# Router products on raw x by token, best two among 8 columns, and a tenth place in the ring

## The chip, the cores and the metric

One Trainium2 chip, of which the kernel uses one core. The metric is the device time of one execution in microseconds (us), lower is better; the kernel before was run three times. A core has TensorE (PE; its weight loads are PEld), VectorE (DVE), ScalarE (ACT), GpSimd (POOL) and SyncE (SP), which only issues transfers here, and 16 DMA engines. All data are float32.

## The reference

One layer of a decoder for 256 prompt tokens and 8 sample tokens (D = 1024), cut to what the change touches:

```python
x = x + merge_branches(pool_out, att, gate_logits, w_up_pool, w_up_att, w_out)
h = rmsnorm(x, norm_ffn)
gl = h @ w_rg + b_rg                                  # 4 groups
g_idx, g_w = argmax(gl), softmax(gl)[argmax]
el = einsum('nd,gde->nge', h, w_re) + b_re            # 4 x 8 experts
el_sel = el[:, g_idx]                                 # the 8 of the chosen group
top_v, top_i = top_k(el_sel, 2); top_w = softmax(top_v)
gate = g_w * one_hot(g_idx) * sum(top_w * one_hot(top_i))
for w1, w3, w2, ge in 32 experts:
    acc += ge * ((silu(h @ w1) * (h @ w3)) @ w2)
y = rmsnorm(x + acc, norm_final)
```

Ahead of it stand an input projection (u, q, k, v, forget logits and 16 gate blocks of 128 columns), a pooling branch, attention over the prompt, and for each sample token attention over 1024 cached rows read through a page table.

## The kernel before

The weights pass through a ring of nine places of 2 MB (`slot`, one `ring` tensor). In the first part places 0 to 5 hold the input projection's weights, key pages (K), value pages (V), the up projections and w_out; 6 to 8 hold working tensors. `PLAN` is one list of steps that all engines walk in the same order, each doing its own share of a step: `proj` and `gate` (projection blocks on PE, copied out by ACT), `keys` (32 steps on DVE: one product with the broadcast query L1004 and one sum L1006 each, four for each sample token), `scores`, `smax`, `hnorm`, `pT`, `pv` (prompt attention), `snew` (the new key of the samples), `m1`, `dmax`, `dshift` (maximum over pages), `dpv`, `datt` (sample attention), `up`, `merge`, `out` (w_out), `norm` and `route`. What a step loads into a place is issued when the last use of its predecessor is over: by SP for weights and for the query broadcasts `qb`, by POOL for pages (`gather_pages`), in the order of the list. POOL also packs the router weights `wre`, `wrg` into `wr`, behind the step `psum` 3, when the five loads that ACT issues in `router_loads` (step `nat` of V) are in.

After `out`, for x of blocks 0 and 1 (128 tokens each) and the sample block 2: squares and root on ACT (L682, L687), a refinement of the root (L883 to L887) and `h2 = x * root` on DVE (L891), transposes of `h2` on PE (L1291, L1294), copies with the norm weights into `hT` on DVE (L904), router products with `wr` as the loaded side, 36 x tokens (L1584, L1591), bias on DVE, transposes back to tokens (L1598), then `route`: argmax over 4 groups, a mask of -1e30 on the experts of other groups, two rounds of argmax over 32 columns (`first_of_equals`, L1093 to L1097, five dependent instructions on 3 x 32 columns), ranks of the tokens in their experts by products with a triangle of ones (L1608), the first token gather (L1316). `inject` (L1306, L1308) puts x into the output accumulators in PSUM; `keep_warm` (L1369) is a product whose result nobody reads.

Then 32 experts: gather the tokens, transpose them, gate and up products (L1333), hidden values, down products (L1349), return to the tokens. Expert e uses places 3(e mod 3) to 3(e mod 3) + 2. SP loads the nine matrices of experts 0 to 2 as the places come free, in the order `FREED` of their last use, and further ones when the gate and up (`s_gu`) or the down products (`s_dn`) of expert e - 3 are done. Expert 31's matrices come in parts, and a final norm ends the kernel.

## Time and profile before

| | us |
|---|---|
| three runs | 736.56, 735.04, 734.88 (median 735.04) |
| profiled execution, whole | 734.89 |
| its span | 733.1 |
| PE busy in the span | 602.4 (82%) |
| DVE busy | 226.0 (31%) |
| ACT busy | 83.8 (11%) |
| POOL busy | 47.3 (6%) |
| moved by DMA | 269.13 MB, mean 367 GB/s |
| matrices of experts, 2048 KB each | 96 |

The span is the profiled stretch of the core; 1.8 us of the execution lie around it. Busy time of PE is not a measure of its being the limit, as products are pipelined; the slices, the stretches, the queue of SP and the chain of work that ended last (followed back from the last instruction to what released each one) say what each part waits for. In a timeline a row is a run of like instructions, with the idle time ahead of it and its releaser in brackets.

### The profile page before, as it was taken

What the parts mean: (1) busy time and instruction counts of PE and PEld (TensorE: products, weight loads), DVE (VectorE), ACT (ScalarE), POOL (GpSimd) and SP (SyncE); (2) the same over time, 40 slices, a digit from 0 to 9 for tenths busy, and PEclk for the clock granted to TensorE, in tenths of its full rate; (3) what the DMA queues carried; (4) which work ended last, traced back from release to release, by engine and by line L of the source; (5) the groups of instructions that cost most, each with busy time, mean ns of one, the idle gap of its engine ahead of it and who ended that gap; (6) DMA issues with size and microseconds to landing.
All of it is one profiled execution on the core that took longest, in us unless ns stands there. A gap on an engine that the chain in (4) does not pass through costs nothing.

```text
span 733.1 us, 13747 instructions
## 1 busy us (share of the span) xinstructions
PE 602.4 (82%) x6164; PEld 368.6 (50%) x6164; DVE 226.0 (31%) x550; ACT 83.8 (11%) x224; POOL 47.3 (6%) x58
## 2 busy tenths in 40 slices
PE   4899999999999999998667786778767676778774
PEld 3678777775574455554334443344334343444342
DVE  4249689972131462321111111111111111111113
ACT  2211142221101201000000000000000000000003
POOL 4106430112000000000000000000000000000000
PEclk8799999999999999999888898778988898889898
DMA  9967969997999456999999999999999999999992
GB/s 299 301 249 242 251 245 396 295 398 306 414 422 414 169 234 250 426 428 425 422 421 426 427 422 422 427 425 424 425 426 426 424 422 426 425 425 422 424 371 91
DMA packets 36602, 269.13 MB, mean 367 GB/s; under 512 B 5076, under 2 KB 5896, under 8 KB 18103
## 3 DMA queue, kind: packets, MB, share of 16 engines
q1 hardware_dynamic: 29824, 230.91, 78.4%
q0 software_dynamic: 3072, 35.19, 11.9%
q10 hardware_dynamic: 3647, 2.14, 1.0%
q8 instruction: 50, 0.82, 0.4%
q14 instruction: 9, 0.07, 0.0%
HBM read 265.99 MB, written 2.46 MB: 366 GB/s over the span
## 4 chain that ended last, share of the span: by engine, by line
DMA 49%; PE 47%; DVE 1%; ACT 1%; issue 1%; SPq 0%; ACTq 0%; DVEq 0%
DMA ring<-w_up 46%; PE bank L1333 9%; PE bank L1416 8%; PE bank L1508 8%; PE bank L1554 4%; PE bank L1569 4%; DMA wf<-w_in 3%; PE bank L1485 2%; PE bank L1349 1%; PE bank L1316 1%; PE bank L1364 1%; PE bank L1492 1%; PE bank L1369 1%; PE bank L1519 1%; PE bank L1523 1%
## 5 line engine op out<-in xcount | busy, mean ns | idle before, releaser
L1333 PE MATMUL bank<-ring,front 128*32 128x256 f32 x2048 | 163.4, 489 | 100.6 <-DMA ring<-w_up 97.0
L1333 PEld LDWEIGHTS bank<-ring,front 128*32 128x32 f32 x2048 | 89.7, 139 | 166.6 <-issue 142.6
L1192 DVE COPY front<-bank 128x256 f32<-128x256 f32 x32 | 13.6, 425 | 241.7 <-PE bank L1333 241.7
L1349 PE MATMUL bank<-ring,front 128*32 128x256 f32 x1024 | 61.2, 379 | 0.0
L1416 PE MATMUL bank<-hT,ring 128*128 128x264 f32 x256 | 60.9, 398 | 0.0
L1508 PE MATMUL bank<-hT,ring 128*128 128x264 f32 x256 | 59.7, 389 | 0.4 <-ACT front L758 0.4
L1416 PEld LDWEIGHTS bank<-hT,ring 128*128 128x128 f32 x256 | 49.5, 196 | 9.9 <-issue 1.2
L1316 PE MATMUL bank<-front 128*32 128x256 f32 (+1 forms) x768 | 53.0, 390 | 0.3 <-DVE front L1103 0.3
L1508 PEld LDWEIGHTS bank<-hT,ring 128*128 128x128 f32 x256 | 47.8, 190 | 9.7 <-issue 2.1
L815 ACT ACTIVATE front<-bank 128x128 f32<-128x128 f32 x32 | 8.9, 277 | 377.1 <-PE bank L1341 377.1
L1349 PEld LDWEIGHTS bank<-ring,front 128*32 128x32 f32 x1024 | 33.1, 110 | 22.1 <-issue 0.5
L1004 DVE TENSOR_TENSOR ring<-ring,front 128x1024 f32<-128x1024 f32 x32 | 40.4, 1263 | 4.3 <-DMA front<-q_scratch 4.2
L1202 DVE COPY front<-bank 128x256 f32<-128x256 f32 x32 | 13.6, 424 | 86.7 <-PE bank L1349 86.7
L1006 DVE TENSOR_REDUCE front<-ring 128x16 f32<-128x1024 f32 x32 | 39.0, 1220 | 1.1
L1364 PE MATMUL bank<-front 32*128 32x256 f32 x512 | 36.7, 400 | 0.0
L1316 PEld LDWEIGHTS bank<-front 128*32 128x32 f32 (+1 forms) x768 | 18.4, 108 | 24.7 <-issue 18.6
L1364 PEld LDWEIGHTS bank<-front 32*128 32x128 f32 x512 | 23.1, 184 | 13.9 <-issue 13.2
L1569 PE MATMUL bank<-ring,hT 128*128 128x512 f32 x64 | 28.3, 597 | 0.0
L1197 DVE TENSOR_TENSOR front<-front,bank 128x128 f32<-128x128 f32 x32 | 9.2, 287 | 41.8 <-ACT front L815 41.8
L1358 PE MATMUL bank<-front 128*32 128x256 f32 x256 | 20.0, 380 | 1.1 <-DVE front L1202 1.1
L1569 PEld LDWEIGHTS bank<-ring,hT 128*128 128x128 f32 x64 | 11.9, 190 | 16.4 <-issue 16.4
L820 ACT COPY front<-bank 128x256 f32<-128x256 f32 x32 | 11.9, 372 | 45.0 <-PE bank L1316 45.0
(293 smaller groups left out, 488.2 us busy)
## 6 DMA issues: line engine op xcount, KB each, us to landing
ring<-w_gate SPq DMA_DIRECT2D x31, 2048.0 KB, 33.8
ring<-w_down SPq DMA_DIRECT2D x31, 2048.0 KB, 38.5
ring<-w_up SPq DMA_DIRECT2D x31, 2048.0 KB, 38.3
ring<-w_in SPq DMA_DIRECT2D x8, 2048.0 KB, 22.9
ring<-w_out SPq DMA_DIRECT2D x2, 2048.0 KB, 16.8
front<-q_scratch SPq DMA_DIRECT2D x8, 256.0 KB, 7.8
ring<-w_up_pool SPq DMA_DIRECT2D x1, 2048.0 KB, 30.5
ring<-w_up_att SPq DMA_DIRECT2D x1, 2048.0 KB, 15.7
```

Of the source, the lines that this page charges most:

```text
L1004: v.tensor_tensor(ks, ks, qb[:, b % 2].unsqueeze(1).to_broadcast([P, 2, DC]), ALU.mult).then_inc(s_kprod, 1)
L1006: v.tensor_reduce(scs[:, b, 2 * pair:2 * pair + 2], ks.rearrange("p j (h d) -> p j h d", h=HEADS), AX.X, ALU.add).then_inc(s_kused, 1)
L1316: last = m.matmul(bank[GATHER][CAP * g:CAP * (g + 1), 0:QUART], sel[0:n, i, b], h2[0:n, b, g * QUART:(g + 1) * QUART], start=b == 2, stop= ...
L1333: last = m.matmul(bank[GATEUP][32 * g:32 * g + 32, 0:256], xgT[:, k % 2, k // 2], w[:, k, 256 * (g % 2):256 * (g % 2) + 256], start=k == 0 ...
L1349: last = m.matmul(bank[TDOWN][32 * g:32 * g + 32, 0:256], hE[:, j % 2, j // 2], wd[:, j, 256 * g:256 * g + 256], start=j == 0, stop=j == F ...
L1358: last = m.matmul(bank[SACC][CAP * g:CAP * (g + 1), 0:QUART], back[:, i, SEQ + CAP * g:SEQ + CAP * (g + 1)], ysb[:, i], start=False, stop= ...
L1364: last = m.matmul(acc[:, g, b], back[rows, i, b * P:(b + 1) * P], ysb[rows, i], start=False, stop=False, skip_group_check=True)
L1416: last = m.matmul(out[:, 0:TOK], w, hT[:, k, 0:TOK], start=k == 0, stop=k == DK - 1)
L1485: last = m.matmul(out[g:g + HEADS, :], scs[:, a, j], pages[:, j], start=j < 4, stop=j >= 4)
L1508: last = m.matmul(out[:, 0:TOK], w[:, k, cols], hT[:, k, 0:TOK], start=k == 0, stop=k == DK - 1)
L1554: last = m.matmul(out[:, 0:TOK], w[:, k, a * P:(a + 1) * P], src[:, k], start=k == 0, stop=k == CC - 1)
L1569: last = m.matmul(out[:], hT[:, k, b * P:(b + 1) * P], w[k // CC][:, k % CC, half * 512:(half + 1) * 512], start=k == 0, stop=k == DK - 1)
```

## The change

- **Ring.** `x` moves into a tenth place of 4096 columns (`x9`), together with `samp`, `unew` and the scratch for squares. After x is injected and normalised, that place takes expert matrices. Places are handed out in the order `FREED`, matrix n to place n mod 10; matrix n waits for the use of matrix n - 10. The final norm's results go into a place that is no longer needed.
- **Router.** x itself is transposed, among the products with w_out, and copied by ACT (one quarter by DVE). The router weights are loaded with rows (k p), in runs of 8 and 4 floats, and multiplied by the norm weights on POOL; they are now the moved side, so that logits stand by token. Root and bias are applied behind the product. ACT writes `h2` of block 1.
- **Choice.** The 8 logits of the chosen group are selected into 8 columns, both argmax rounds run on 3 x 8 columns, and the results are spread over 32 again. `turned(0)` stands earlier. Sample rows are 8 instead of 128 in rank and table products.
- **Order ahead of it.** `forgetT` one projection later; the product of new keys split off (`sprod`) ahead of `snew`; key steps one earlier. The query broadcasts of sample tokens 2 to 7 are issued by ACT at the second key step of the token before, no longer by SP. One more small load for the norm weights.

```diff
-NSLOT = 9
-NB = NSLOT // 3
+RING = 9
+NSLOT = RING + 1
+LAST = EXPERTS - 1
+ORDER = [(e, m) for e in range(LAST - 1) for m in range(3)] + [(LAST - 1, 0), (LAST - 1, 1), (LAST, 0), (LAST, 1), (LAST - 1, 2), (LAST, 2)]
...
+        x9 = sb("x9", [P, SLOT])
+        slot = [ring[:, n * SLOT:(n + 1) * SLOT] for n in range(RING)] + [x9[:]]
+        x = x9[:, 0:3 * D].rearrange("p (b n) -> p b n", b=3)
+        samp, unew = x9[:, 3 * D:3 * D + DC], x9[:, 3 * D + DC:4 * D]
...
-        PLAN += V[:1] + [("nat", C_K)] + keys(2)[:1] + V[1:2] + [("snew", 0)] + keys(2)[1:2] + V[2:3] + [("scores", 0)] + keys(2)[2:] + V[3:] + [("smax", 0)]
+        PLAN += V[:1] + [("nat", C_K), ("sprod", 0)] + keys(2)[:2] + V[1:2] + keys(2)[2:] + [("snew", 0)] + V[2:3] + [("scores", 0)] + keys(3)[:1] + V[3:] + [("smax", 0)]
-        KEYS_AT = (12, 13, 15, 17, 18, 19, 21, 23, 25, 26, 28, 30, 31, 32)
+        KEYS_AT = (13, 14, 16, 18, 19, 20, 22, 24, 26, 27, 28, 30, 31, 32)
...
+        home = {item: FREED[n % NSLOT] for n, item in enumerate(ORDER)}
+        arrived = {item: SLOT_BASE[home[item]] + 16 * (n // NSLOT + 1) for n, item in enumerate(ORDER)}
...
+                elif q == 8:
+                    sp.wait_ge(s_merge, DK)
                 else:
-                    sp.wait_ge(s_merge, DK)
-                load_matrix(sp, q // 3, q % 3, q)
+                    sp.wait_ge(s_inj, 1)
+                    sp.wait_ge(s_h2, 1)
+                load_matrix(sp, *ORDER[n], q)
+            def slot_used(n):
+                e, m = ORDER[n - NSLOT]
+                sp.wait_ge(s_gu if m < 2 else s_dn, e + 1)
...
-                    pool.wait_ge(in_route, 16 * 5)
-                    g.tensor_copy(wr[:, :, 0:EXPERTS].rearrange("p k (g e) -> p k g e", g=GROUPS), wre[:].rearrange("p g (k e) -> p k g e", k=DK)).then_inc(s_wr, 1)
-                    g.tensor_copy(wr[:, :, EXPERTS:], wrg[:].rearrange("p (k g) -> p k g", k=DK)).then_inc(s_wr, 1)
+                    pool.wait_ge(in_route, 16 * (GROUPS + 4))
+                    pool.wait_ge(*count_taken("pool"))
+                    g.tensor_tensor(wr[:], wr[:], nffnK.unsqueeze(2).to_broadcast([P, DK, EXPERTS + GROUPS]), ALU.mult).then_inc(s_wr, 1)
...
-                act.dma_start(wre[:], t["w_router_expert"][0].rearrange("g (p k) e -> p g (k e)", p=P)).then_inc(in_route, 16)
-                act.dma_start(wrg[:], t["w_router_group"][0].rearrange("(p k) g -> p (k g)", p=P)).then_inc(in_route, 16)
+                for g in range(GROUPS):
+                    act.dma_start(wr[:, :, g * PER_GROUP:(g + 1) * PER_GROUP], t["w_router_expert"][0, g].rearrange("(k p) e -> p k e", p=P)).then_inc(in_route, 16)
+                act.dma_start(wr[:, :, EXPERTS:], t["w_router_group"][0].rearrange("(k p) g -> p k g", p=P)).then_inc(in_route, 16)
...
+                elif step == "keys" and a % 4 == QROW_AT and a // 4 + 1 in range(2, NS):
+                    b = a // 4 + 1
+                    act.wait_ge(s_kprod, 4 * (b - 1))
+                    act.dma_start(qb[:, b % 2], qd[b].partition_broadcast(P)).then_inc(s_qb[b % 2], 16)
...
                 elif step == "norm":
...
+                    for half in range(2):
+                        s.copy(hT[:, 4 * half:4 * half + 4, 0:P], full("hT", 1 + half)[:].rearrange("p (k t) -> p k t", k=4)).then_inc(taken[TPOSE[1 + half][0]], 1)
...
+                    act.wait_ge(s_hsum, 1)
+                    s.activation(root[:, 1], rowsq[:, 1], ACT.Sqrt, bias=eps).then_inc(s_rt, 1)
+                    act.wait_ge(s_hsum, 2)
+                    s.activation(h2[:, 1].rearrange("t (k p) -> t p k", k=DK), x[:, 1].rearrange("t (p k) -> t p k", k=DK), ACT.Copy, scale=root[:, 1]).then_inc(s_h2, 1)
...
             def route():
                 src = full("logits")
-                link(v.memset(lgT[0:36, TOK:3 * P], 0.0))
-                v.tensor_scalar(lgT[0:36, 0:TOK], src[0:36, 0:TOK], br[:, 0:1], None, ALU.add).then_inc(taken[PART], 1)
+                v.scalar_tensor_tensor(lg[:, 1], src[:, 0:36], root[:, 1], br[:], ALU.mult, ALU.add).then_inc(taken[PART], 1)
...
-                first_of_equals(e1, em, r_m1, EXPERTS, ra)
-                link(v.scalar_tensor_tensor(em, e1, -2 * BIG, em, ALU.mult, ALU.add))
-                first_of_equals(e2, em, r_m2, EXPERTS, ra)
+                link(v.tensor_tensor(ra.rearrange("p b (g e) -> p b g e", g=GROUPS), lg[:, :, 0:EXPERTS].rearrange("p b (g e) -> p b g e", g=GROUPS), by_group, ALU.mult))
+                link(v.tensor_reduce(em8, ra.rearrange("p b (g e) -> p b e g", g=GROUPS), AX.X, ALU.add))
+                first_of_equals(first8, em8, r_m1, PER_GROUP, ra8)
+                link(v.scalar_tensor_tensor(em8, first8, -2 * BIG, em8, ALU.mult, ALU.add))
+                first_of_equals(top8, em8, r_m2, PER_GROUP, ra8)
...
                         for k in range(DK):
+                            if (i, k) == (3, 4):
+                                transposes(3)
                             last = m.matmul(out[:], hT[:, k, b * P:(b + 1) * P], w[k // CC][:, k % CC, half * 512:(half + 1) * 512], start=k == 0, stop=k == DK - 1)
...
+                        if i == 2:
+                            for block in range(1, 3):
+                                transposes(block)
+                            transposes(0)
                 elif step == "norm":
...
+                    for k in range(DK):
+                        m.matmul(out0[:, 0:36], hT[:, k, 0:P], wr[:, k], start=k == 0, stop=k == DK - 1)
...
+                    transposes(4)
+                    transposes(5)
...
+                    for k in range(4, DK):
+                        last = m.matmul(out[:, 0:36], xT1[:, k], wr[:, k], start=False, stop=k == DK - 1)
...
                 elif step == "route":
                     pe.wait_ge(*count_taken("datt", NS - 1))
                     keep_warm(CHAIN, 4)
+                    inject()
                     pe.wait_ge(*count_taken("logits"))
-                    for b in range(3):
-                        last = m.transpose(out[:, 36 * b:36 * b + 36], lgT[0:36, b * P:(b + 1) * P], ident[0:36, 0:36])
-                    last.then_inc(filled[SUM], 1)
-                    inject()
                     keep_warm(PART, 4)
-                    keep_warm(PART, 2)
```

## Rows read from the trace of the kernel before

**Rows 1.** Page, part 2: GB/s moved, in 40 slices of 18.33 us.

```profile
GB/s 299 301 249 242 251 245 396 295 398 306 414 422 414 169 234 250 426 428 425 422 421 426 427 422 422 427 425 424 425 426 426 424 422 426 425 425 422 424 371 91
```

**Rows 2.** Stretches: length, busy PE, PEld, DVE, ACT, POOL, then PEclk, DMA, GB/s.

```profile
245.00:250.00 5.00, 5.00 (x13) 2.26 (x12) 2.70 (x3) 0.00 (x0) 0.00 (x0) 1.00 0.07 28
275.00:280.00 5.00, 5.00 (x62) 3.11 (x66) 1.96 (x9) 1.53 (x2) 0.00 (x0) 0.83 0.01 3
282.60:718.00 435.40, 333.19 (x4624) 183.18 (x4620) 68.06 (x227) 21.61 (x64) 0.00 (x0) 0.87 1.00 420
```

**Rows 3.** Timeline of SyncE, 250 to 282 us: start us, us, instruction.

```profile
253.88 0.80 SPq L477 DMA_DIRECT2D ring<-w_up  x2
280.71 0.33 SPq L477 DMA_DIRECT2D ring<-w_gate  x1
```

**Rows 4.** Chain of work that ended last: start us, us, engine, tile, line, instructions.

```profile
93.19 3.56 PE bank L1508 x16
...
253.85 0.59 PE bank L1291 x8
254.44 0.60 PE bank L1294 x4
...
264.37 3.67 PE bank L1306 x8
...
268.61 1.49 PE bank L1369 x4
270.18 1.51 PE bank L1608 x12
```

**Rows 5.** By line and form, 254 to 285 us: count | busy, mean ns.

```profile
L1584 PE MATMUL bank<-hT,wr 128*36 128x8 f32 x16 | 0.7, 179 | 0.0
...
L1094 DVE TENSOR_TENSOR hT<-hT 128x96 f32<-128x96 f32 x2 | 0.5, 258 | 0.1
...
L1094 DVE TENSOR_TENSOR hT<-hT 128x12 f32<-128x12 f32 x1 | 0.2, 173 | 0.0
```

**Rows 6.** Waits of TensorE, 20 to 256 us: us in total, times, longest.

```profile
PE bank L1462 <- ACT front L728: 0.7, 1, 0.7
```

**Rows 7.** Timeline of GpSimd and of ScalarE's DMA issues, 75 to 103 us.

```profile
75.24 1.48 POOL L604 DMA_INDIRECT ring<-cache_k,ridx  x1 [3.71 <-PE bank L1416]
...
102.09 0.39 POOL L649 COPY wr<-wre 128x256 f32<-128x256 f32 x1 [18.50 <-DMA br<-b_router_group]
...
99.18 0.45 ACTq L710 DMA_DIRECT2D wre<-w_router_expert  x1
```

**Rows 8.** Timeline of VectorE, 83 to 162 us; the page's row of L1004.

```profile
83.75 0.23 DVE L991 COPY front<-bank 128x64 f32<-128x64 f32 x1 [6.28 <-PE bank L1445]
...
107.56 1.21 DVE L1004 TENSOR_TENSOR ring<-ring,front 128x1024 f32<-128x1024 f32 x1
...
161.84 0.28 DVE L1013 TENSOR_REDUCE stat<-bank 64x1 f32<-64x128 f32 x1 [0.46 <-PE bank L1475]
...
L1004 DVE TENSOR_TENSOR ring<-ring,front 128x1024 f32<-128x1024 f32 x32 | 40.4, 1263 | 4.3 <-DMA front<-q_scratch 4.2
```

**Rows 9.** DMA queues, 6-10 us, then 98-102 us: packets, MB, share.

```profile
q1 hardware_dynamic: 332, 1.36, 99.9%
q10 hardware_dynamic: 261, 0.01, 3.8%
...
q10 hardware_dynamic: 872, 0.15, 19.6%
```

**Rows 10.** Issues with us to landing, from 253.5, 104.1, 89.5 and 74.5 us.

```profile
ring<-w_up SPq DMA_DIRECT2D x1, 2048.0 KB, 8.7
...
ring<-cache_k,ridx POOLq DMA_INDIRECT x1, 10.0
...
front<-q_scratch SPq DMA_DIRECT2D x1, 256.0 KB, 10.3
...
ring<-w_in SPq DMA_DIRECT2D x1, 2048.0 KB, 24.0
```

More of the change, by code:

```diff
@@ new lines, in _ @@
+                    mean_square(2, NS, sqmoe)
+                    for i in range(2):
+                        act.wait_ge(*count_taken("out", i))
+                    mean_square(0, P, sqmoe)
+                    square_root(slice(0, 3, 2), 4)
+                    for half in range(2):
+                        s.copy(hT[:, 4 * half:4 * half + 4, 0:P], full("hT", 1 + half)[:].rearrange("p (k t) -> p k t", k=4)).then_inc(taken[TPOSE[1 + half][0]], 1)
+                    s.copy(hT[:, :, SEQ:TOK], full("hT", 0)[:, 0:DK * NS].rearrange("p (k t) -> p k t", k=DK)).then_inc(taken[TPOSE[0][0]], 1)
@@ L1581, in _ @@
+                    pe.wait_ge(s_wr, 1)
+                    for i in range(1, 3):
                         pe.wait_ge(*count_taken("hT", i))
[L1582 to L1585 removed]
+                    for k in range(DK):
+                        m.matmul(out0[:, 0:36], hT[:, k, 0:P], wr[:, k], start=k == 0, stop=k == DK - 1)
@@ new lines, in _ @@
+                    pe.wait_ge(*count_taken("hT", 0))
+                    for k in range(DK):
+                        last = m.matmul(out0[0:NS, 36:72], hT[:, k, SEQ:TOK], wr[:, k], start=k == 0, stop=k == DK - 1)
+                    last.then_inc(filled[SUM], 1)
+                    transposes(4)
+                    transposes(5)
+                    pe.wait_ge(*count_taken("hT", 3))
+                    for k in range(4):
+                        m.matmul(out[:, 0:36], xT1[:, k], wr[:, k], start=k == 0, stop=False)
```

306 lines of the change are left out of this document (144 added, 162 removed).

## Prediction, written before the result was known

> **What bounds the kernel now.** I read the moved bytes by slice first [rows 1]: from the 17th slice (293 us) to the 38th every slice moves 421 to 428 GB/s, and just ahead of them three slices fall to 169, 234 and 250. The stretches [rows 2] say why. At 245 to 250 us and 275 to 280 us the DMA engines are busy 0.07 and 0.01 of the time while TensorE is busy throughout; from 282.6 to 718 us the DMA share is 1.00 and TensorE works 333 of 435 us. SyncE's queue [rows 3] joins the two: two expert matrices are issued at 253.88, when the last product with w_out has freed their places, and the next only at 280.71, when expert 0's gate and up products have freed a place. In between all nine places of the ring are full. So there are two regimes. Up to the end of expert 0's first products the time is TensorE's (with VectorE's routing chain in it), and the memory waits; behind it the time is the memory's. The end is
>
> (end of expert 0's gate and up products, now 280.7) + (matrices not yet loaded) x (time of one) + tail.
>
> 96 - 9 = 87 matrices of 2 MB go through in 435.4 us: **5.0 us each**. Whatever shortens only work behind 282.6 us is worth nothing; what ends the front earlier counts in full, and each matrix loaded in the idle stretch takes 5.0 us off the second term.
>
> **The tenth place.** It removes one matrix from the 87: **-5.0 us**. Its load is issued when the injection of x into the accumulators and ScalarE's normalised second block are done, by the sum below near 267. Into an idle memory a load took 8.7 us from issue to landing [rows 10]: landed by 276, or 277 if the final norm's 0.5 MB (1.2 us at 425 GB/s) goes first. The first products end near 278 and release the following loads, so it fits with 1 to 2 us to spare; should it start later, every us beyond that is lost, up to 5.0.
>
> **The stretch between w_out and the experts.** Now, in the chain of work that ended last [rows 4]: the last w_out product ends at 253.85, the sums over the earlier tokens (ranks) start at 270.2, expert 0's first products end at 280.7. The part behind 270.2 (ranks, gather, turn, products) is nearly unchanged: 10.5 us. For the part ahead of it I lay out TensorE:
> - Transposes of raw x are put among the w_out products: 12 of 128x128 at 0.60/4 = 0.15 us, 8 of 8 rows 0.59 us [rows 4]. Added: 2.4 us, so w_out ends at 256.25. (Before, they were behind it, with waits for VectorE ahead of and behind each set.)
> - Router products by token: 128 columns of weights loaded, 36 moved. The trace has this form as 128x32, 12 in 1.51 us, 0.126 us each [rows 4]; 16 for block 0 are 2.0 us. The 16 of the sample tokens load 8 columns and move 36; not shown. Nearest is the same product with the sides swapped, 0.7 us for 16 [rows 5]; the other bound is 2.0. I take 0.9. The two transposes that wait for the last half of block 1 (0.55 us; x is added up some 0.7 us after 256.25, covered by block 0's products), then 16 products, 2.0. Sum: 261.7. The copies for them are halves of 256 columns, hidden behind the first four.
> - One warming product (1.0 us), the injection (264.37 to 268.61 now, 4.2 us), another warming one (some two thirds of 1.49, 0.9) [rows 4]: 267.8.
> - VectorE: bias and root applied, 0.5 us; then the choice of experts. Now it runs ten dependent operations on 96 columns at 0.26 us; on 24 columns they should cost what 12 columns do, 0.17 us [rows 5], with one reduction more and one or two fewer masks: 4.5 us instead of 5.4. From 261.7 the choice is ready at 266.7. That is 1.1 us before TensorE gets to the ranks, so **the 8-column search is worth nothing here**: the injection hides it. If it took over 1.1 us more than I sum, or the root of block 1 came later than 262, each further us would count.
> Ranks start at 267.8 instead of 270.2: **-2.4 us**. Bounds: -1.3 with 2.0 us for the sample products; -3.5 if these take their 0.7 and the second warming one is done in the time of the choice. The removed logits copy, 36-row transposes and their round trip are in this difference; the earlier turned(0) is worth nothing, since VectorE's first 128-row products are not late now. Fewer rows in ranks and table products load no fewer columns: nothing.
>
> **Ahead of w_out.** TensorE runs with few gaps here. It waits in 21 to 256 us for ScalarE's copy before the forget transposes (L1462, 0.7 us) [rows 6]; that step moves one projection later, and 0.6 us of it should go. I take **-0.6 us**, bounds 0 and -2.6 (all such waits).
>
> Sum: -5.0 - 2.4 - 0.6 = -8.0, of which I give back 0.5 for TensorE waiting at the new places (copy of the sample block, banks): **-7.5 us**. The profiled execution took 734.9 us (span 733.1); it gives 727.4, and the median of the three runs (735.04) 0.1 more: **727.5 us**.
>
> **What may eat this: the router's loads.** They change from long runs to runs of 8 and 4 floats. ScalarE issues them one after the other (the second at 99.18) and GpSimd, in order, waits for the last of them until 102.09 before it sends its next page gather [rows 7]. Before: 872 packets on that queue in 98 to 102 us. After: 4 x 1024 runs of 32 B, 1024 of 16 B, some 400 others: 5,500. The cost of one is in the forget weights' load at the start, also runs of 32 B: 261 packets in 6 to 10 us took 3.8% of 16 engines, 9 ns each [rows 9]. At that, 5,500 take 3.2 us on 16 engines, less than issuing them (8 issues at the 0.45 us of the second or somewhat more, up to 103). The other bound is the pace at which those 261 got through beside 332 large packets, 65 per us: 85 us. I take the first, since the memory is all but idle at 98 to 102 us (19.6% for this queue). The loads then land near 106, 4 us later than now. Behind them stand: on ScalarE's queue the query of sample 4, wanted for the 17th product with pages (107.56 now), and on GpSimd's the gather of the keys of sample 5, 10.0 us from issue to landing [rows 10].
> VectorE's order says what may be late. It now idles 6.28 us at 83.75 for the new keys' product; with the product split off, it runs a step (2.4 us: the product 1.26, the sum behind it about as much) further ahead from there on, and waits for queries sum to 4.2 us [rows 8]. At 161.84 it had waited 0.46 us for TensorE's transpose of the page maxima, a transpose that itself needs VectorE: the two are level, and lateness beyond the new lead of 2.4 us moves the whole front. The 17th product would now start at 105.2; its query, issued at 103, needs 3 to 10 us.
>
> **Rivals.**
> B, the query comes late. The query of sample 4 needed 10.3 us from SyncE's queue, behind a weight load [rows 10]; from ScalarE's at 103 it would land at 113, 8 late, less the lead of 2.4 and 0.5: 5 us of TensorE waiting, mean of the cases 3. **730.5 us**. For: the small packets stand ahead of it. Against: the weight load no longer does. The Trainium skill speaks for B: "Trainium Kernel Development and Optimization", section Key Constraints, says that DMAs from SyncE, ScalarE and GpSimd share the same 16 engines and that issuing from several saves issue time only. By that rule the query keeps its 10.3 us and the time is 732.
> C, small runs pace the kernel: **slower**. If 5,500 packets pass at 65 per us, the queue is clear at 184, the query is 79 us late and the front ends 75 us later: 802 us. The change turns slower than before once VectorE is more than 2.4 + 0.5 + 7.5, some 10 us late at the 17th product, which is when the queue is not clear until about 115. Against: the large packets beside them are one weight load of 1024. The Trainium skill, "DMA: Bandwidth & Descriptors", section Why small descriptors are slow, also says that each descriptor carries a fixed overhead; the 9 ns above is the trace's figure for it.
> D, the first gate weights come late. Their place is now one that the last key projection frees; GpSimd's gather at 75.24 waited for that projection [rows 7], and gate 0 starts at 93.19 [rows 4]. A load of such weights beside two page gathers took 24.0 us [rows 10], which would be 99; with one gather I estimate 17 (92). Late by 0 to 5 us, mean 2.5: **730.0 us**.
> E, the tenth place or the stretch before the experts gives half: 731 us where the load is late by 4, 730 where TensorE's stretch saves nothing. **730.3 us**. For: my margins of 1 to 2 us there. Against: the load needs no more than 8.7 us.
> F, "it doesn't do what it says": the stretch from 282.6 us stays as long, since it depends on some other limit than bytes. Then the 5.0 are lost: 732.4. Against: DMA share 1.00 at 425 GB/s.
>
> **How the numbers follow.** A (the forecast) 0.62, B 0.14, C 0.05, D 0.07, E 0.08, F 0.04. A measurement of this kernel tells about 0.3% from no change, 2.2 us, so faster is below 732.8. All of A, D, E and most of B and F are: faster 0.89, same 0.06 (B with its full 5 us and something of D), slower 0.05 (C). Range: below, 725.3 (w_out stretch -3.5, all front waits gone); above, 732.0, which takes in B, D and E but for their tails.
>
> **What would show it.** The gap in SyncE's loads: two issues near 256, one near 267, next at 278; then 86 matrices at 5.0 us. VectorE's routing chain shorter, but TensorE's ranks starting when warming ends. At 98 to 107 us a short burst of small packets, the 17th product at 105 to 108. Wrong would be: ranks waiting for VectorE; the page-maxima transpose later than 161; gate 0 waiting for its weights; a gap in the memory's share after 280.

## The result

The changed kernel takes 724.21 us (median of 4 runs, 723.57 to 725.64), the one before, beside it, 734.96 (734.66 to 736.56): ratio 0.984, 95% interval 0.981 to 0.988. The gain is 10.75 us, where 7.5 were forecast, and the time lies 1.1 us below the low end of the range. The profiled execution took 723.92 us, its span 721.9, against 733.1: 11.2 us. The kernel before, executed 66 more times beside the experiments, took 733.0 to 736.7 us in 50 of them and 738.3 to 742.7 in the other 16.

The page of the changed kernel, part 2, in slices of 18.05 us (granted clock of TensorE in tenths; busy share of the DMA engines in tenths; GB/s):

```profile
PEclk9999999999999999999888987799888988789898
DMA  9965989997999489999999999999999999999982
GB/s 300 303 260 203 347 146 402 359 377 300 414 422 414 199 313 366 425 426 419 424 427 427 422 422 429 427 423 421 426 427 424 423 424 424 428 425 424 422 368 88
```

The two slices behind the drop to 199 move 313 and 366 GB/s, where [rows 1] has 234 and 250. SyncE's queue in the changed kernel (start us, us, instruction) shows with what:

```profile
254.69 0.33 SPq L488 DMA_DIRECT2D ring<-w_up  x1
255.06 0.44 SPq L490 DMA_DIRECT2D ring<-w_down  x1
264.28 0.33 SPq L488 DMA_DIRECT2D x<-w_gate  x1
274.42 0.33 SPq L488 DMA_DIRECT2D ring<-w_up  x1
```

Between the issue at the end of w_out and the next one [rows 3] had 26.8 us; now there are 9.2 and 10.1 us, with the matrix for x's place between them. Stretches of the changed kernel (length, busy PE, PEld, DVE, ACT, POOL, then PEclk, DMA share, GB/s), to be held against the second and third of [rows 2] (the last 5 us of the second one are already the end of the kernel, which is why it has 415 GB/s and not 420):

```profile
264.00:274.00 10.00, 9.57 (x114) 5.51 (x110) 5.50 (x27) 3.34 (x6) 0.00 (x0) 1.00 0.93 367
276.40:711.80 435.40, 338.37 (x4689) 185.25 (x4682) 68.98 (x230) 22.50 (x67) 0.00 (x0) 0.87 0.99 415
```

The stretch ahead of the experts, TensorE (start us, us, line, instruction):

```profile
254.50 1.87 PE L1618 MATMUL bank<-wr,hT 128*128 128x36 f32 x16
256.30 0.69 PE L1621 MATMUL bank<-wr,hT 128*8 128x36 f32 x16
256.92 0.66 PE L1325 MATMUL bank<-cea,x 128*128 128x128 f32 x4
257.41 0.98 PE L1627 MATMUL bank<-wr,front 128*128 128x36 f32 x8
258.22 1.06 PE L1631 MATMUL bank<-wr,front 128*128 128x36 f32 x8
259.11 1.10 PE L1399 MATMUL bank<-cea 128*128 128x512 f32 x2
260.06 3.60 PE L1337 MATMUL bank<-x,cea 128*128 128x512 f32 x8
...
265.11 0.30 PE L1644 MATMUL bank<-hT,cla 128*128 128x32 f32 x2
...
270.69 3.66 PE L1363 MATMUL bank<-ring,front 128*32 128x256 f32 x64 [0.22 <-DVE front L1138]
```

It has no gap over 0.1 us from w_out's last product to the gather. So the 11.2 us are, by four marks that every profile has (first product with w_out; first product of the ranks; first gate and up product of expert 0; VectorE's copy behind the last of these; end): 1.29 us ahead of w_out, 3.78 from w_out's start to the ranks (w_out's stage is 2.10 longer, the rest 5.88 shorter), 1.23 from the ranks to the products, 4.90 behind these. The forecast for the same four was 0.6, 1.9 (2.4 less the 0.5 given back for waits at the new places), 0 and 5.0. The last holds; the other three carry the miss, 0.7, 1.9 and 1.2.

### The profile page after: what moved, and what is told of

It is laid out like the page before. It is cut to its first block, busy times and chain, and to the rows that moved or that the text cites. A ratio compares the mean times of both kernels' runs of the same rounds, so it can differ in the third digit from the quotient of the medians.

```text
span 721.9 us, 13750 instructions
## 1 busy us (share of the span) xinstructions
PE 599.4 (83%) x6157; PEld 367.1 (51%) x6157; DVE 223.3 (31%) x549; ACT 88.3 (12%) x232; POOL 51.1 (7%) x57
## 4 chain that ended last, share of the span: by engine, by line
PE 50%; DMA 46%; DVE 1%; ACT 1%; issue 1%; ACTq 0%; DVEq 0%
DMA ring<-w_up 33%; PE bank L1363 10%; PE bank L1446 8%; PE bank L1538 8%; DMA x<-w_up 5%; DMA ring<-w_down 5%; PE bank L1584 4%; PE bank L1601 4%; DMA wf<-w_in 3%; PE bank L1379 2%; PE bank L1515 2%; PE bank L1347 2%; PE bank L1394 1%; PE bank L1522 1%; PE bank L1388 1%
## 5 line engine op out<-in xcount | busy, mean ns | idle before, releaser
L1363 PE MATMUL bank<-ring,front 128*32 128x256 f32 x1856 | 162.7, 486 | 85.8 <-DMA ring<-w_up 73.8
L1363 PEld LDWEIGHTS bank<-ring,front 128*32 128x32 f32 x1856 | 86.6, 138 | 144.9 <-issue 120.6
L1379 PE MATMUL bank<-ring,front 128*32 128x256 f32 x928 | 55.4, 379 | 0.2 <-DMA ring<-w_down 0.2
L1019 DVE TENSOR_TENSOR ring<-ring,front 128x1024 f32<-128x1024 f32 x32 | 41.9, 1310 | 8.1 <-DMA front<-q_scratch 7.7
L1379 PEld LDWEIGHTS bank<-ring,front 128*32 128x32 f32 x928 | 30.2, 110 | 20.2 <-issue 0.8
L1363 PE MATMUL bank<-x,front 128*32 128x256 f32 x192 | 31.6, 502 | 8.7 <-DMA ring<-w_up 8.1
L1363 PEld LDWEIGHTS bank<-x,front 128*32 128x32 f32 x192 | 14.7, 143 | 15.9 <-issue 13.6
```

The costliest lines, as they stand in the source:

```text
L1019: v.tensor_tensor(ks, ks, qb[:, b % 2].unsqueeze(1).to_broadcast([P, 2, DC]), ALU.mult).then_inc(s_kprod, 1)
L1363: last = m.matmul(bank[GATEUP][32 * g:32 * g + 32, 0:256], xgT[:, k % 2, k // 2], w[:, k, 256 * (g % 2):256 * (g % 2) + 256], start=k == 0 ...
L1379: last = m.matmul(bank[TDOWN][32 * g:32 * g + 32, 0:256], hE[:, j % 2, j // 2], wd[:, j, 256 * g:256 * g + 256], start=j == 0, stop=j == F ...
```

## The experiments

Timings of one kernel spread over 2 to 9 us, so verdicts below rest on stretches of the traces, and times are given beside them. From w_out to the products the stretches repeat to 0.1 us where the clock is the same; the start of w_out and the part behind the products don't, with 4 us (217.25 to 221.61) and 2.9 us (447.1 to 450.0) between profiles that have the same order of work there. All marks of all profiles, in us (gather: duration of the first 24 gather products, 1.64 with the granted clock held, more where it fell to 0.5):

| kernel | w_out starts | from there to ranks | ranks to products | gather | behind products | median of runs |
|---|---|---|---|---|---|---|
| before | 219.96 | 50.22 | 6.81 | 2.35 | 452.4 | 734.96 |
| before again (n4) | 220.72 | 50.22 | 6.72 | 1.64 | 452.0 | 735.28 |
| before, copy early (n11) | 220.25 | 50.22 | 5.52 | 1.64 | 452.4 | 734.24 |
| before, forget later (n16) | 222.26 | 50.23 | 6.94 | 2.48 | 454.0 | 739.73 |
| changed | 218.67 | 46.44 | 5.58 | 1.64 | 447.5 | 724.21 |
| changed again (n9) | 220.21 | 46.44 | 5.59 | 1.64 | 447.5 | 725.70 |
| nine places (n1) | 217.25 | 46.44 | 5.59 | 1.63 | 452.9 | 729.27 |
| 32 columns (n2) | 218.49 | 46.44 | 6.88 | 2.31 | 448.5 | 726.96 |
| no filling (n3) | 219.75 | 45.86 | 6.94 | 2.26 | 449.0 | 725.88 |
| copy back (n10) | 221.61 | 46.44 | 6.80 | 1.64 | 448.9 | 726.92 |
| products twice (n12) | 220.78 | 48.22 | 6.70 | 1.97 | 450.0 | 728.48 |
| old order (n8) | 222.87 | 46.44 | 5.58 | 1.64 | 447.4 | 728.77 |
| queries on SyncE (n6) | 217.80 | 46.44 | 5.59 | 1.64 | 447.1 | 724.33 |
| router late (n13) | 224.45 | 46.44 | 5.59 | 1.64 | 448.9 | 731.16 |
| and no filling (n14) | 223.85 | 45.86 | 5.67 | 1.63 | 447.5 | 730.46 |
| behind exp (n15) | 218.65 | 46.44 | 5.59 | 1.64 | 447.4 | 725.87 |
| and no filling (n17) | 218.02 | 45.86 | 7.16 | 2.57 | 447.9 | 724.86 |

### The tenth place

```diff
-        home = {item: FREED[n % NSLOT] for n, item in enumerate(ORDER)}
+        home = {item: FREED[n % RING] for n, item in enumerate(ORDER)}
```

> The changed kernel with one part undone: the ring of expert weights has its nine places again and the place in x stays empty. Theory (the tenth place gives what the traces show behind expert 0's first products, 452.4 us before and 447.5 us after): the stretch from the end of the injection to expert 0's products is unchanged, within 0.3 us, and all of the loss stands behind it, +4.9 us, so 729 us against 724.2. Rival (the ring is full again soon, and the place only starts a transfer sooner that another would have filled): under 2 us. Rival (contention: the added transfer slows the x and selection work of 264 to 274 us): then that stretch gets shorter here by some 0.5 us and the loss is under 4.5.

729.27 us (727.76 to 730.71), and 452.9 us behind the products instead of 447.5; the stretch ahead of them is the same to 0.01 us. SyncE's four issues of the last matrix's parts begin 399.9 us behind the products, with ten places 395.0: 4.9 us, one matrix. Neither rival is seen.

### The search over 8 columns

The mask over 32 columns comes back with it, and the selection and the spreading go.

```diff
-                first_of_equals(first8, em8, r_m1, PER_GROUP, ra8)
...
-                first_of_equals(top8, em8, r_m2, PER_GROUP, ra8)
+                first_of_equals(e1, em, r_m1, EXPERTS, ra)
...
+                first_of_equals(e2, em, r_m2, EXPERTS, ra)
```

> The changed kernel with the search for the best two experts among 32 columns again, instead of 8. Theory (the injection and the products that keep TensorE's clock up hide the search; its result was ready 0.7 to 0.9 us ahead of its reader): VectorE's chain grows by about 0.9 us (before, its operations on 96 columns against 24), so the ranks' products start 0 to 0.3 us later and the kernel takes 724.2 to 724.6. Rival (VectorE's chain is what the ranks wait for, and TensorE's filling products only seem to end last): the ranks start 0.9 us later and the kernel takes 725.1.

The ranks start 46.44 us behind w_out's start, as with 8 columns: the search is hidden, which is the first theory, though by little. VectorE's choice is ready 0.3 us before the ranks here, 0.7 with 8 columns. 726.96 us (723.4 to 728.05) is no evidence against it: in the profile the clock fell in the gather, with the same instructions on TensorE as in the changed kernel:

```profile
267.27 2.31 PE L1345 MATMUL bank<-front 8*32 8x256 f32 x24 [0.18 <-DVE front L1130]
...
271.81 3.66 PE L1361 MATMUL bank<-ring,front 128*32 128x256 f32 x64
```

### The filling products ahead of the injection

```diff
                     pe.wait_ge(*count_taken("datt", NS - 1))
-                    keep_warm(CHAIN, 4)
                     inject()
```

> The changed kernel without the four filling products ahead of the injection (about 1.05 us of TensorE). Theory A (TensorE's order is what ends last between the logits and the ranks, and the clock stays at its upper level without them): the injection ends about 1 us sooner, the tenth place's transfer starts 1 us sooner, the ranks start as soon as the search is ready, 0.7 to 0.9 us sooner, and the kernel takes 723.3. Theory B (those products are what holds the clock): the granted clock falls to 0.5 for some 2 us between 258 and 278 us as in the kernel before, the gather takes 2.4 us instead of 1.6, and the kernel takes 724.2 to 725.6.

The ranks come 0.58 us sooner, less than the 0.94 that the products took: now VectorE's result is what ends last. And the clock fell in the gather (2.26 us), 1.36 us lost. 725.88 us (723.54 to 727.57): nothing gained. That their absence brings the clock down isn't shown: without them it fell in two profiles of three (n3 and n17, not n14), with them in one of ten and partly in one more (n2, n12).

### The kernel before once more

> The kernel before once more, nothing changed, for a second profile of it: which of its stretches at the lower clock come back. Theory A (the low clock at 274 to 276 us belongs to its order of work, which leaves TensorE idle between w_out and the ranks): it comes back, with a gather of some 2.35 us and 10.5 us from the ranks to expert 0's first products. Rival (it is chance): this profile has 1.00 there and 9.1 us. The same question for 14 to 27 us, where both kernels have the same instructions on TensorE: if this profile has 1.00 there, the change's 1.0 us ahead of 29 us is chance and no part of it.

The low clock of 14 to 27 us came back (0.50), that of 272 to 278 did not. But the stretch from the ranks to the products is as long as before, 6.72 against 6.81, so there the clock is not where the time went.

The early stretch is another matter. Of the 1.29 us that the changed kernel is ahead at w_out, 1.00 has arisen by a product of TensorE that starts at 28 to 29 us (29.02 at L1457, 28.02 at L1487), before any step that the change reorders. The 16 products just ahead of that step, in the kernel before (clock 0.50 up to 27 us) and in the changed one (1.00):

```profile
23.30 5.88 PE L1416 MATMUL bank<-hT,ring 128*128 128x264 f32 x16
```

```profile
23.38 4.80 PE L1446 MATMUL bank<-hT,ring 128*128 128x264 f32 x16
```

In the six profiles with 0.50 up to about 27 us (the three of the order before, n8, n12 and n15) they took 5.60 to 5.94 us, in the eleven where the clock was back by 25 us or never down 4.38 to 5.51, and that product came at 28.3 to 29.2 us against 27.1 to 28.5. Both kernels have profiles of both kinds (n16 has the edited order of before and 1.00), so most of that 1.0 us goes with the clock that an execution got, or with the arrival of its first weights, and no run shows that the change has a part in it.

What TensorE waits for from the ranks to the products (268 to 281 us, in this second profile) stood in no row of the first:

```profile
PE bank L1333 <- DVE front L1112: 1.4, 1, 1.4
PE bank L1316 <- DVE front L1103: 0.3, 1, 0.3
```

L1112 is `turned(0)`, the copy of expert 0's turned tokens, which the change puts between the two columns of VectorE's slot work. VectorE's last row ahead of the products and TensorE's first, in the profile of [rows 1 to 10]:

```profile
276.45 0.49 DVE L1112 TENSOR_TENSOR front<-bank,nffn 128x128 f32<-128x128 f32 x2
...
276.99 3.66 PE L1333 MATMUL bank<-ring,front 128*32 128x256 f32 x64
```

The products begin 0.05 us behind the copy's end. TensorE shows no wait only because its filling products ran at the low clock and ended as late.

### The copy of the turned tokens, put back and made alone

```diff
                     link(v.tensor_tensor(wE, wE, selE[:, :, c, 1], ALU.add))
-                    if c == 0:
-                        turned(0)
...
+                turned(0)
```

> The changed kernel with one line undone: the turned tokens of expert 0 are again copied behind both columns of VectorE's slot work, where before the change they stood, and no longer between the two. Theory (the earlier copy is what shortened the stretch from the ranks to expert 0's products: the second profile of the kernel before has TensorE waiting 1.43 us there for this copy, 6.7 us in all against 5.6): with the clock held the stretch is 6.7 us, TensorE waits 1.1 to 1.4 us for the copy, and the kernel is 1.1 us slower; with the clock down in the gather it is 6.9 either way, since TensorE's slower products then end as late as the copy. Rival (the copy is hidden, and the difference of the two kernels there was the clock alone, as I had it in the prediction): no wait, 5.6 us with the clock held.

> The kernel before with this one line of the change alone: the copy of expert 0's turned tokens moved between the two columns of VectorE's slot work. Theory: the stretch from the ranks to expert 0's products goes from 6.7 to 5.6 us if the granted clock holds, and the kernel from 734.9 to 733.8; if the clock falls in the gather, it stays at 6.8 to 6.9. Rival (nothing, as predicted): 6.7 or 6.8 in both cases.

The first products of expert 0: changed kernel with the copy back, then kernel before with the copy early.

```profile
274.85 3.66 PE L1362 MATMUL bank<-ring,front 128*32 128x256 f32 x64 [1.43 <-DVE front L1138]
```

```profile
275.99 3.66 PE L1334 MATMUL bank<-ring,front 128*32 128x256 f32 x64 [0.22 <-DVE front L1112]
```

With the clock held in both, the stretch is 6.80 with the copy back against 5.58, and 5.52 with it early against 6.72: the one line is 1.2 us in either kernel, on and off. The time of the kernel before with this line early is 734.24 us, ratio to before 0.994 (0.990 to 0.998). That ratio is no measure of the line: eight of the thirteen executions of before beside it took 739.8 to 742.7 us, and only two of these ten took over 736. Of the executions under 737 us the medians are 733.9 (8) and 735.5 (5), 1.6 us apart, which fits 1.2. 726.92 us (725.89 to 729.92) with it back is 1.2 above the changed kernel on the same chip, within its spread. The rival, "nothing, as predicted", falls.

### The path from w_out to the ranks

```diff
+                    for _ in range(2):
                         for k in range(DK):
-                        m.matmul(out0[:, 0:36], hT[:, k, 0:P], wr[:, k], start=k == 0, stop=k == DK - 1)
+                            m.matmul(out0[:, 0:36], hT[:, k, 0:P], wr[:, k], start=k == 0, stop=k == DK - 1)
```

> The changed kernel with the 16 router products of block 0 done twice; the result is the same. They took 1.81 us from start to start, where I had summed 2.0. Theory (TensorE's order is the path from w_out to the ranks): the ranks start 1.8 us later behind w_out, 12.25 us instead of 10.45, and the kernel takes 1.8 us more. Rival (VectorE's work for the root and the logits of block 1 ends last): less than 1 us.

The stretch grows by 1.78 us, all of what the products take: TensorE's order is the path here. 728.48 us (725.32 to 734.18); beyond the 1.8 us this profile also has the clock down behind the gather and at the end.

### The order ahead of w_out

```diff
-[("nat", C_Q)] + U[1:2] + [("forgetT", 0)] + U[2:3] + [("bias", 0)] + keys(0)[:1]
+[("nat", C_Q), ("forgetT", 0)] + U[1:2] + [("bias", 0)] + U[2:3] + keys(0)[:1]
...
-V[:1] + [("nat", C_K), ("sprod", 0)] + keys(2)[:2] + V[1:2] + keys(2)[2:] + [("snew", 0)]
+V[:1] + [("nat", C_K)] + keys(2)[:1] + V[1:2] + [("sprod", 0), ("snew", 0)] + keys(2)[1:2]
```

> The changed kernel with the order of steps ahead of w_out as before (the forget transposes one projection earlier, the product of the new keys directly ahead of their sum, the key steps one place later), all else as changed. Theory 1: the 0.66 us that TensorE waited ahead of the forget transposes comes back. Theory 2 (that order is what pays for the late queries: VectorE waited 3.07 us for that of sample 4 and still was only 0.24 us late at the maximum over pages): VectorE loses a lead of about 2.4 us, the maximum over pages comes 2 to 3 us late, and the start of w_out goes from 217.3 to 219.8 us to about 222; the kernel takes 727 to 728. Rival (VectorE catches up elsewhere): only the 0.7 us.

The edit shows parts of two lines of `PLAN`; the later key steps go back by one as well. w_out starts at 222.87, 3.3 us behind the mean of the seven profiles that have the changed kernel's order and loads up to there (217.25 to 221.61, mean 219.54). TensorE's waits from 20 to 254 us:

```profile
PE bank L1561 <- DVE front L1068: 1.6, 1, 1.6
PE bank L1505 <- DVE front L1026: 0.9, 1, 0.9
PE bank L1584 <- DVE ring L1048: 0.7, 1, 0.7
PE bank L1492 <- ACT x L740: 0.7, 1, 0.7
```

The 0.7 us ahead of the forget transposes (L1492) are back: the first theory holds. Of the rest, 1.15 us have arisen by the product at 28 to 29 us (29.22 against a mean of 28.07), where the order is still the same. VectorE is late at the transposes behind the values (L1561) and at the maximum over pages (L1505), but so it is in one profile of the changed order (n10: 1.8 and 0.9 us). For the second theory speak the times: 728.77 us (727.92 to 731.51), all four above the changed kernel's four on the same chip (n9, 724.13 to 727.06). That the old order is slower, by some 3 us in these executions, is shown; that it is by VectorE's lead, and by which of the three moves undone here, is argued.

The first step alone, in the kernel before:

```diff
-[("nat", C_Q), ("forgetT", 0)] + U[1:2] + [("bias", 0)] + U[2:3]
+[("nat", C_Q)] + U[1:2] + [("forgetT", 0)] + U[2:3] + [("bias", 0)]
```

> The kernel before with the forget transposes one projection later, nothing else. Theory (this step of the prediction): the wait of 0.66 us ahead of them, there in three profiles of three, goes, and w_out starts at 219.3 to 220.1 instead of 220.0 to 220.7: 0.6 us gained. Rival (VectorE is level with TensorE at the maximum over pages and takes it back there): the wait before that maximum's transpose grows from 0 to 0.7 us to 0.7 to 1.3, and nothing is gained.

Slower: 739.73 us, ratio 1.006 (1.003 to 1.008). All ten executions took 739.07 to 741.79, where of the seventeen of before beside it fourteen took 733.62 to 736.20 and three 739.51 to 740.38. So the edit makes the rule what the kernel before does at times by itself; no profile of it at that level exists, so whether it has the same cause there is open. The 0.7 us at L1462 are gone and more than given back, w_out starts at 222.26 against 220.3:

```profile
PE bank L1531 <- DVE front L1053: 2.2, 1, 2.2
PE bank L1584 <- DVE hT L904: 1.0, 1, 1.0
PE bank L1475 <- DVE front L1011: 0.9, 1, 0.9
```

```profile
151.13 1.23 DVE L1004 TENSOR_TENSOR ring<-ring,front 128x1024 f32<-128x1024 f32 x1 [4.97 <-DMA front<-q_scratch]
```

VectorE waits 5.0 us for one query at 151 us, and TensorE 3.1 us for VectorE at its two meeting points (L1531, L1475). That query took 19.8 us from issue to landing, in two profiles of the kernel before 16.3 and 17.1. The rival was right with its wait ahead of the page maxima (0.9 us), and the 2.2 us at L1531 come on top. Another 1.7 us are lost behind the products, where the last 24 us ran at a mean clock of 0.78 against 0.88; why is open.

### The router's small loads and the queries

```diff
                     if a == C_V:
-                        router_loads()
...
                 elif step == "dshift":
+                    router_loads()
                     act.wait_ge(*count_taken("dshift", 0))
                     s.activation(scs, scs, ACT.Exp).then_inc(s_pex, 1)
...
+                elif step == "out":
                     pool.wait_ge(in_route, 16 * (GROUPS + 4))
```

> The changed kernel with the router's small loads issued by ScalarE some 60 us later (at the shift by the maximum over pages, about 162 us), so behind all queries but the last ones, and GpSimd's multiplication of the router weights moved from about 105 us to the step of w_out, so that GpSimd's page gathers no longer queue behind it. Theory (the small loads, ahead of the query of sample 4 on ScalarE's queue and ahead of the page gather of sample 5 on GpSimd's, are what takes VectorE's lead): VectorE's 3.1 us wait for the query of sample 4 and its 0.4 to 2.5 us wait for the keys of sample 5 go, TensorE no longer waits for the maximum over pages (0 to 1.8 us in the profiles so far), and w_out starts at 217.3 to 218.7, the lowest values so far, against a mean of 219.3: 0 to 1.5 us gained, 724 us. Rival 1 (the waits are those of any query issued so late): they stay, 725. Rival 2 (small packets at 162 us hold up the weights of w_out or the value pages): TensorE waits for transfers ahead of w_out, and it is slower.

> The same with the four filling products ahead of the injection gone as well. They took 0.94 us of TensorE, of which 0.58 us came off the stretch from w_out to the ranks when left out alone (9.87 against 10.45). Theory: both gains add, 0.6 us below the kernel with the router's loads late, if the granted clock holds; with the clock down in the gather 1.3 us more. Rival: leaving them out is what brings the clock down in the gather (it was down in the one profile without them), so that nothing is gained.

Slower than the changed kernel, 731.16 (728.67 to 732.72) and 730.46 us (728.36 to 734.22), by a cause in neither rival. ScalarE's timeline in n13:

```profile
164.64 3.92 ACTq L723 DMA_DIRECT2D wr<-w_router_expert  x4
168.59 0.65 ACTq L724 DMA_DIRECT2D wr<-w_router_group  x1
...
170.40 0.68 ACT L765 ACTIVATE front<-front 128x576 f32<-128x576 f32 x1 [5.75 <-issue]
```

The eight issues take 6 us, and the exponential of the page scores queues behind them; TensorE waits 4.0 us for its sums (3.6 in n14). The next kernel issues them behind it:

```diff
                     s.activation(scs, scs, ACT.Exp).then_inc(s_pex, 1)
+                    router_loads()
```

> As the kernel with the router's loads late, but the eight loads stand behind the exponential of the page scores on ScalarE's queue and not ahead of it (there TensorE's row sums waited 4.0 us for that exponential). Theory (the small loads at 97 to 102 us cost VectorE its lead, nothing else was wrong with moving them): the 4.0 us wait is gone, VectorE's waits stay at 5.5 us with none for the query of sample 4 above 1 us, TensorE does not wait for the maximum over pages, w_out starts at 217.3 to 219, and the kernel takes 722.5 to 724.5. Rival (the small loads hold up the weights of w_out or the value pages where they now stand): TensorE waits for a transfer ahead of w_out, 726 or more.

> The same without the four filling products ahead of the injection. Theory: 0.6 us faster than with them (9.87 us from w_out's end to the ranks instead of 10.45), 722 to 724. Rival (the granted clock falls in the gather more often without them): 1.3 us slower where it does, so on the whole slower than with them. The clock held in one of two profiles without them, and in seven of eight of the other kernels with the changed routing.

The 4.0 us are gone, TensorE never waits at L1561 or L1505 (in four of the seven profiles mentioned it did, 0.9 to 2.7 us), and w_out starts at 218.65 and 218.02. What remains of VectorE's wait for the query of sample 4, in the changed kernel and in n15:

```profile
106.85 1.23 DVE L1019 TENSOR_TENSOR ring<-ring,front 128x1024 f32<-128x1024 f32 x1 [3.07 <-DMA front<-q_scratch]
120.63 1.23 DVE L1019 TENSOR_TENSOR ring<-ring,front 128x1024 f32<-128x1024 f32 x1 [0.42 <-DMA ring<-cache_k,ridx]
```

```profile
105.98 1.23 DVE L1019 TENSOR_TENSOR ring<-ring,front 128x1024 f32<-128x1024 f32 x1 [1.84 <-DMA front<-q_scratch]
```

Over all profiles the wait for this query is 2.2 to 3.6 us with the small loads where the change has them (seven, mean 3.1) and 1.8 to 2.6 with them later (four, mean 2.2), so they account for about 0.9 us of it. The wait for the keys of sample 5 (0.4 to 2.5 us in the seven) is in none of the four. The query isn't held up on its way: it landed 4.4 us after its issue in the changed kernel and 9.0 in n13. The small loads delay its issue, from 97.7 to 102.3 us, since ScalarE's queue is busy with them for 5 us. Against the mean start of w_out of 219.5 the two kernels are 0.9 and 1.5 us ahead, which two profiles and times of 725.87 (723.67 to 731.24) and 724.86 us (723.99 to 725.99) bear out as a direction only: in time neither differs from the changed kernel.

```diff
-                elif step == "keys" and a % 4 == QROW_AT and a // 4 + 1 in range(2, NS):
-                    act.dma_start(qb[:, b % 2], qd[b].partition_broadcast(P)).then_inc(s_qb[b % 2], 16)
...
-ready = {("q", b): PLAN.index(("nat", C_Q)) for b in range(2)}
+ready = {("q", b): PLAN.index(("keys", 4 * b - 5)) if b >= 2 else PLAN.index(("nat", C_Q)) for b in range(NS)}
```

> The changed kernel with the queries of samples 2 to 7 issued by SyncE at the place in its order that they had before, no longer by ScalarE. Theory (ScalarE's queue lets the query of sample 4 wait behind the router's small loads): that wait of VectorE falls from 3.1 us to 1 us, as in the kernel before, but SyncE's order now issues queries behind weights that wait for a place, so that others grow; together the waits for queries are 2 to 5 us, against 5.8 to 8.8, and w_out starts at 217.5 to 219.5. Rival (ScalarE's queue is the better one): the waits grow over 8 us and w_out starts at 221 or later.

VectorE waits 4.8 us for the query of sample 3, which took 16.4 us to land (3.4 us of waiting and 10.7 in the changed kernel), and 3.3 for the keys of sample 5, none for the query of sample 4; w_out starts at 217.80, within what was expected; 724.33 us (722.57 to 726.81), again no difference in time.

The changed kernel once more, for what is chance:

> The changed kernel once more, nothing changed, as a second profile of it. Of the stretches where single profiles differ, this one should show which are the kernel's and which are chance. The kernel's own (theory): from the ranks to expert 0's gate and up products 5.6 us when the granted clock holds and 6.9 when it falls to 0.5 in the gather; behind the end of those products 447.5 us, within 0.5. Chance: the start of w_out, which stood at 217.3, 218.7 and 219.8 us in three profiles with the same order of work there. Time 724 to 727.

The stretches are the same to 0.05 us, and w_out starts 1.54 us later, with TensorE waiting 0.9 us at L1505 and 0.4 at L1561. So the part ahead of w_out is the one that differs from execution to execution. 725.70 us (724.13 to 727.06).

## Why the prediction was off

**Two regimes, the end set by the end of expert 0's first products: right.** The part behind them is 447.1 to 450.0 us in all profiles with ten places, wherever the products end (273.5 to 280.1 us), and each matrix took the 5.0 us.

**Tenth place, -5.0: right.** 4.9 us. Its load was issued at 264.3, not near 267, since the stretch ahead was shorter, and had 10.1 us until the products' end.

**From w_out to the ranks, -2.4 less the 0.5 given back: mechanism right, sizes off.** Measured -3.78. The 0.5 for waits at the new places had no row behind it, and there is no such wait. w_out's stage grew by 2.10 instead of 2.4. The 16 products of block 0 took 1.80 us from start to start, not 2.0, and those of block 1 1.70: I had taken 0.126 us each from twelve short products of another form [rows 4]. The 16 of the sample took 0.62; the nearer row [rows 5] has 0.7, and I put 0.9. My low bound for this term, -3.5, was set with only the sample's and the warming product's price varied; the ones that I took as known were the larger part. The low end of the range, 725.3, doesn't follow from the bounds either: with -3.5 here and -2.6 ahead of w_out the same sum gives 724.4, which the measured 724.21 would have missed by 0.2.

**The 8-column search, nothing: right.** VectorE's operations on 24 columns took 0.18 us where I put 0.17, the choice was ready 0.7 us before TensorE came to it, and 32 columns made no difference to the ranks. The Trainium skill, "VectorE: DVE Perf Modes", section The TRN2 errata, says that operations on data in SBUF pay a fixed cost per instruction, and gives (N + 151) / 0.96 GHz for a float32 addition of two tensors of N columns: an estimate of 0.18 us for 24 columns and 0.26 for 96. The traces agree (0.18 and 0.26), which is why a quarter of the columns saves a third of the time.

**"The earlier turned(0) is worth nothing, since VectorE's first 128-row products are not late now": wrong, and the step that failed.** It was put at nothing and is worth 1.2 us; with it the forecast would have been 726.3, and its range would have held the result. The sentence rested on there being no row in which TensorE waits for this copy. But in that profile its filling products ran at the low clock, up to the very moment at which the copy ended; at the full clock it waits 1.43 us. A missing wait was read as slack, where the copy's end and the products' start were 0.05 us apart. The same sight made the whole stretch behind the ranks "nearly unchanged".

It also shows how the low clock hides what it costs: in the kernel before a fall in the gather costs 0.1 us (6.81 against 6.72), since VectorE's copy ends as late; in the changed one 1.3 (6.88 against 5.58).

**Ahead of w_out, -0.6: small and uncertain, as put, for a reason half seen.** The mean starts are 220.3 (three profiles of the order before) and 219.5 (seven of the changed): 0.8 us where 0.6 were forecast, so the 1.29 of the first two profiles is partly chance, and the nearness of the 0.8 is luck. By the product at 28 to 29 us, ahead of all that the change reorders, the means already differ by 1.0 (29.05 and 28.07); from there to w_out it is 191.3 against 191.5 us. TensorE's wait at L1462 went, as forecast, and lateness of VectorE took it back (0.9 to 2.7 us in four of the seven). That this step is worth 0.6 by itself was wrong: alone it made the kernel 4.7 us slower. That VectorE and TensorE are level behind it, and that the gain needs the lead from the split product, fits both n16 and n8, but no run undoes the split alone.

**Rival B, the late query: it occurred, in small.** The Trainium skill's rule spoke for it ("Trainium Kernel Development and Optimization", section Key Constraints: issuing from several engines saves issue time only). The times agree with it, 724.33 us with SyncE issuing and 724.21 with ScalarE. What I drew from it, that this query keeps its 10.3 us, did not come: it landed 4.4 us after its issue. It was late by 3.1 us of VectorE's time because the issue itself stood behind eight small ones. The longest wait, 3.4 us, was for the query of sample 3, which no small load stood ahead of and which the prediction didn't look at. TensorE's waits for VectorE behind it were 0 to 2.7 us and not 5. The queries' waits rose from 4.2 us in all [rows 8] to 7.7.

**Rival C, small runs that pace the kernel: not seen.** The DMA queues of the changed kernel from 98 to 102 us (packets, MB, share of 16 engines):

```profile
q10 hardware_dynamic: 4417, 0.14, 58.7%
q1 hardware_dynamic: 56, 0.10, 6.3%
```

That is 8.5 ns a packet on 16 engines, where I had taken 9 from [rows 9]. **Rival D** was not seen: gate 0 started at 91.7 and waited for nothing. **E and F** did not occur.

**What stays open.** Why the clock falls in the gather in some executions and not in others; why moving the forget transposes alone makes the last 24 us slower; what the kernel before does in the 16 of 66 executions that took 738 us and more; and whether any of the 0.8 us ahead of w_out is the change's, with starts that spread over 4 us.

## What to carry to other kernels

A wait that isn't in the profile is no slack: before writing "hidden", subtract the end of the work from the start of its reader, and ask whether the reader was itself slowed, by the clock for instance. Where two engines are level, a saving on one may be worth nothing; so price such edits together, and run them alone as well. When two profiles differ, look first at whether they already differ ahead of the first thing that was changed. And when a term is summed from several products, vary the price of each for the range, not only of the one that is unknown.

## What the hardware did that I had not expected

- The granted clock differs between executions of the same instructions: the first gather took 1.64 us in one profile of the kernel before and 2.35 in the other, and stretches with a level of 0.5 came and went in the same way in the changed kernel.
- At 14 to 20 us a clock of 0.50 cost nothing, since TensorE has no product there: the kernel with nine places had it, had the upper clock back at 24 us, and came to the product behind its first weights at 27.1 us, the changed kernel at 28.0. Where 0.50 lasted until 27 us, the 16 products at 23 us took 5.60 to 5.94 us, elsewhere 4.38 to 5.51.
- Four loads of the router weights took ScalarE's queue 2.8 us to issue at 97 us and 3.9 us at 164 us; eight such issues (6 us) ahead of one short operation made TensorE wait 4.0 us.
